# Reordered attention and delta-rule groups, and a last down panel in halves, in a two-layer decoder trunk

## The chip, the cores and the metric

The kernel runs on one core of one Trainium2 chip. The metric is the device time of one execution in microseconds, as the median of several. A profiled execution gives the trace: every instruction with its engine, start, duration, line and tiles, and what ended the idle time before it. The core has TensorE (matmuls, out of which results come in PSUM), VectorE, ScalarE, GpSimd (called POOL) and SyncE, which here issues the DMA transfers.

## What is computed

Two post-norm layers on 256 tokens of width 2048, in float32. Layer 0 mixes tokens by latent attention (12 heads, causal, low-rank queries and keys plus a rotary part), layer 1 by a chunked gated delta rule (12 heads, a short causal convolution on q, k, v). In both, 4 further heads attend to 256 memory tokens. One output projection takes all 16 heads, then come a norm, a squared-ReLU MLP of width 8192 and another norm.

```python
for i in range(2):
    mem_kv = mem @ mem_w_kv[i]
    h = x @ (mla_w_in if i == 0 else gdn_w_in)
    mix = mla_mixer(...) if i == 0 else gdn_mixer(...)      # 12 heads of 128
    mem_o = memory_attention(q_mem, mem_kv)                 # 4 heads of 128
    y = jnp.concatenate([mix, mem_o], -1) @ w_out[i]        # 2048 x 2048
    x = layer_norm(ALPHA * x + y, ln1_g[i], ln1_b[i])
    ff = jnp.square(jax.nn.relu(x @ mlp_w1[i])) @ mlp_w2[i] # 2048 x 8192 x 2048
    x = layer_norm(ALPHA * x + ff, ln2_g[i], ln2_b[i])

def gdn_mixer(...):
    qkv = silu(causal_depthwise_conv(h[..., :3 * MIX_WIDTH], conv_w))
    q, k = l2_normalize(q), l2_normalize(k)
    # per chunk of 64 tokens: u, w = solve(I + L, [v * beta, kb * exp(gc)])
    #   v_new = u - w @ state;  o = q_dec @ state + a_qk @ v_new
    #   state = state * g_last + k_dec^T @ v_new
    return rms_norm(o, o_norm) * silu(z)
```

## The kernel before

**Weights.** Every weight goes through the same ring. A chunk is 256 rows by 512 columns (two k-tiles of 128, 512 KB). SyncE loads it into one of four raw slots (`load`), ScalarE copies it to a reduced-precision high part `whi`, VectorE subtracts to get the low part `wlo` (both are called a split, `split` or `feed`), and TensorE multiplies high by high, high by low and low by high. Chunk c is split only when chunk c - 4 has been used (`chunk_used`), and loaded only when the split of chunk c - 4 is done (`lo_ready`). A panel is 512 output columns over all of k, mostly 8 chunks; panels alternate between two halves of PSUM, and `panel_free` says that one has been copied out. `panel_r` gives rows (tokens on partitions) with weights moving, 12 matmuls of 512 columns a chunk; `panel_t` gives columns, 24 matmuls of 256.

**Queues.** The five programs are written out by hand, one in-order queue for each engine, joined by counting semaphores. What stands behind a wait in a queue waits too.

**Layer 0's attention.** The panels qrope (2), qnope, knope, v (3 each, of two chunks) come from the normalised latents. POOL rotates the rotary queries. Then TensorE turns the rotated rows (L703), three times four transposes, each waiting for ScalarE's copy of the one before (`rot_out`), and starts `attention`: 16 heads in a pipeline of 19 steps. Step i has the scores of head i, one chunk of the first two out0 panels from step 5 on (`out0_chunk`), the transposes of head i-2's probabilities (`turn_probs`) and the values of head i-3 (`values`). ScalarE has `probs_out(i-2)`, `exps(i)`, `head_hi(i-3)` and a split; VectorE has `maxima(i)`, `divide(i-1)`, `head_lo(i-3)` and a split. Memory heads come last. out0's chunks take k-tiles in order, so each waits for the head just finished (`o_lo`).

**Layer 1's groups.** Four heads make a group, three groups. For each: panels q, k, v, with a convolution on each (`conv`: ScalarE scales a copy, VectorE adds three taps in 12 instructions of 253 to 255 columns, L1793, ScalarE takes tanh, VectorE multiplies, L1801, and TensorE turns the result back, `conv_turns`, L855); then `gdn(g)`: transposes of k, kb, q, a masked product, six levels of doubling that invert the triangular matrix, w and u, and four state steps (j loop), with the chunks of z and of the next q (or of qm1) put between (`beside`). At its end VectorE normalises the output rows `orow`, waits for POOL's rsqrt, scales them (`or_set`), and TensorE turns them (`turn`, L631). After the third group the memory heads of layer 1 run with six chunks of out1, once all turned rows are split.

**The end.** `mlp` has four groups of 4 up and 4 down panels. The last down panel ends token tile 0 and then tile 1 within each chunk; `last_rows` (VectorE) adds and takes sums, POOL computes the rsqrt of both tiles, VectorE the factors, ScalarE `norm_block` scales and shifts eight pieces of 512 columns, VectorE `finish` multiplies by the gain row and adds the shift row, and SyncE writes each piece out. The gain and shift rows `gb` are loaded last in SyncE's queue (`gain_rows`), after all weights:

```python
            mlp(1, "mlp1")
            sp.wait_ge(sem.z_ready, 3)
            gain_rows(ln2_g[1:2, :], ln2_b[1:2, :])
```

Of the kernel before, what the change touches and what calls it, by code (L numbers as in the profile page):

```python
# [52 lines left out]
PANEL = KT // CK  # L53
GROUPS = FF // D
# [41 lines left out]
def out_chunk(name, u, ci):  # L96


    if u < 2:
        return CHUNK_AT[name] + 2 * ci + u  # L100
    return CHUNK_AT[name] + u * PANEL + ci
# [11 lines left out]
def place(nc):  # L113
# [27 lines left out]
    b.stats, o = at("stats", [P, TT, 4, 6], F32, o)  # L141
# [87 lines left out]
    b.gb, o = at("gb", [P, 2, D], F32, o)  # L229
    b.low, o = at("low", [P, 2 * UP // 2, S], F32, o)  # L230
# [3 lines left out]
class Semaphores:  # L234


    def __init__(self, signal):
# [41 lines left out]
        self.fin = signal("fin")  # L279
        self.c_sum = signal("c_sum")  # L280
# [88 lines left out]
def build(nc, x, mem, positions_, mla_w_in, mla_q_norm, mla_w_uq, mla_kv_norm, mla_w_ukv, gdn_w_in, gdn_conv,  # L369
          gdn_a_log, gdn_dt_bias, gdn_o_norm, mem_w_kv, w_out, ln1_g, ln1_b, mlp_w1, mlp_w2, ln2_g, ln2_b, out):  # L370
    with ExitStack() as ctx:
# [6 lines left out]
        pt_ps, o_ps = quad_ps[1][:, 2, :], quad_ps[1][:, 3, :]  # L378
        block = ctx.enter_context(nc.Block())
# [13 lines left out]
        def _(sp):  # L393
# [48 lines left out]
            def mlp(l, name):  # L442
                c0 = CHUNK_AT[name]
                with sp.Fori(0, GROUPS) as g:
# [6 lines left out]
                    for u in range(UP):  # L451
                        for ci in range(PANEL):
                            load(c0 + (UP + u) * PANEL + ci,
                                 [(lambda slot: b.raw[:, slot],
                                   mlp_w2[l, bass.ds(g * D + ci * CK * P, CK * P), u * CN:(u + 1) * CN]
                                   .rearrange("(t p) n -> p t n", p=P))], g * GCH)

# [15 lines left out]
            for ci in range(PANEL):  # L473
                for u in range(2):
                    load(out_chunk("out0", u, ci), whole(w_out[0], ci * CK, slice(u * CN, (u + 1) * CN)))
# [27 lines left out]
            for j in range(4):  # L503
                for t in range(TT):
                    sp.wait_ge(sem.fin, 2 * j + t + 1)
# [6 lines left out]
        def _(pe):  # L512
# [111 lines left out]
            def turn(g, src, kts):  # L624

                if g >= 2:
                    pe.wait_ge(sem.turn_f, g - 1)
                for i in range(2):
                    for t in range(TT):
                        kt = kts + i  # L630
                        last = nc.tensor.transpose(turn_ps[g % 2][:, (i * TT + t) * P:(i * TT + t + 1) * P],  # L631
# [53 lines left out]
            for i in range(2):  # L685
                panel_r(PANEL_AT["qrope"] + i, CHUNK_AT["qrope"] + 2 * i, 2, b.ch, b.cl, after_turn("cq"), n=6 * ROPE)
            for i in range(3):
                panel_t(PANEL_AT["qnope"] + i, CHUNK_AT["qnope"] + 2 * i, 2, b.ch, b.cl, after_turn("cq"))
            for i in range(3):
                panel_t(PANEL_AT["knope"] + i, CHUNK_AT["knope"] + 2 * i, 2, b.ch[:, 4:8, :], b.cl[:, 4:8, :],  # L690
# [1454 lines left out]
```

## Time and profile before

| | |
|---|---|
| median of 3 runs | 2470.22 us (2469.14 to 2471.08) |
| profiled execution, its own time | 2471.89 us |
| its span, first to last instruction | 2470.1 us |
| TensorE busy | 2384.2 us (97%) |
| mean granted TensorE clock | 0.986 |
| first matmul of the last down panel's end, to the last instruction | 2452.3 to 2470.1 us |

The span is what the views of the trace cover; the execution's own time has 1.8 us around it. A row of a timeline is a start, a duration, the engine, the instruction and, in brackets, the idle time before it and what ended it. The ends of matmuls are modelled, so a stop of TensorE is a little longer from start to start than its row says. The granted clock is 1.0 at 2.4 GHz and 0.5 at 1.2 GHz.

### The profile page before, as it was taken

The numbers are of one execution on the slowest core, as the hardware profiler recorded it, in microseconds if no ns is written. First come the engines' busy times: TensorE is split into PE (matmuls) and PEld (weight loads), VectorE is DVE, ScalarE is ACT, GpSimd is POOL, SyncE is SP. The second block draws the span as 40 slices with busy tenths as digits, with TensorE's granted clock in tenths as the row PEclk, the third lists the DMA queues.
The fourth block names the chain that finished last, engine by engine and source line by source line (L and its number), as shares of the span: only waits on it lengthen the run. The fifth ranks groups of instructions, "written<-read, shape, count | busy, mean of one in ns | idle before, by whom it ended". The sixth has DMA issues, their size and how long they took to land.

```text
span 2470.1 us, 35483 instructions
## 1 busy us (share of the span) xinstructions
PE 2384.2 (97%) x13572; PEld 2078.7 (84%) x13577; DVE 1467.5 (59%) x1550; ACT 1071.8 (43%) x1340; POOL 247.9 (10%) x221
## 2 busy tenths in 40 slices
PE   8999989999999999999999999989899999999997
PEld 7897778888888888889899898978788888888885
DVE  6654567546555556577756757545865554555555
ACT  4455444434444444354535435333443443443443
POOL 0150001001000001000122320310010000000000
PEclk9999999999999999999999999999999999999999
DMA  6662456565566565655424324126455665656654
GB/s 233 188 187 94 137 172 200 199 193 188 192 185 196 192 191 182 200 190 162 137 69 139 108 79 154 60 90 226 140 188 195 184 196 196 187 190 195 188 191 158
DMA packets 234624, 417.10 MB, mean 169 GB/s; under 512 B 23761, under 2 KB 42474, under 8 KB 232938
## 3 DMA queue, kind: packets, MB, share of 16 engines
q1 hardware_dynamic: 233114, 410.73, 52.2%
q10 hardware_dynamic: 1360, 4.19, 0.4%
q8 instruction: 116, 1.90, 0.3%
q14 instruction: 34, 0.28, 0.0%
HBM read 412.77 MB, written 2.10 MB: 168 GB/s over the span
## 4 chain that ended last, share of the span: by engine, by line
PE 48%; issue 40%; DVE 5%; POOL 4%; ACT 2%; DMA 1%; SPq 0%; POOLq 0%; ACTq 0%; DVEq 0%
PE quad L563 10%; PE quad L592 6%; PE quad L590 6%; PE quad L591 6%; PE quad L566 5%; PE quad L534 3%; PE quad L536 3%; PE quad L538 3%; DVE cv L1793 2%; POOL hl L2070 1%; ACT whi L1036 1%; PE quad L947 1%; PE quad L934 1%; DVE wlo L1413 1%; PE quad L944 1%
## 5 line engine op out<-in xcount | busy, mean ns | idle before, releaser
L1413 DVE TENSOR_TENSOR wlo<-raw,whi 128x1024 fp32r<-128x1024 f32 x760 | 979.1, 1297 | 726.1 <-ACT whi L1036 724.0
L1036 ACT ACTIVATE whi<-raw 128x1024 fp32r<-128x1024 f32 x760 | 798.7, 1058 | 979.7 <-PE quad L592 525.8
L563 PE MATMUL quad<-xs,whi 128*128 128x512 f32 x2048 | 649.9, 397 | 7.4 <-DVE xs L1673 3.7
L590 PE MATMUL quad<-whi,hh 128*128 128x512 f32 x1344 | 528.9, 393 | 5.2 <-DVE hl L1548 3.7
L592 PE MATMUL quad<-whi,hl 128*128 128x512 f32 x1344 | 523.8, 390 | 0.0
L591 PE MATMUL quad<-wlo,hh 128*128 128x512 f32 x1344 | 523.5, 390 | 0.0
L566 PEld LDWEIGHTS quad<-xs,wlo 128*128 128x128 f32 x2048 | 386.7, 189 | 91.0
L566 PE MATMUL quad<-xs,wlo 128*128 128x256 f32 x2048 | 403.8, 279 | 0.0
L563 PEld LDWEIGHTS quad<-xs,whi 128*128 128x128 f32 x2048 | 314.6, 190 | 10.0 <-DVE wlo L1413 5.5
L590 PEld LDWEIGHTS quad<-whi,hh 128*128 128x128 f32 x1344 | 252.7, 188 | 60.0 <-issue 7.2
L592 PEld LDWEIGHTS quad<-whi,hl 128*128 128x128 f32 x1344 | 252.5, 188 | 53.1
L591 PEld LDWEIGHTS quad<-wlo,hh 128*128 128x128 f32 x1344 | 252.7, 188 | 51.8
L534 PE MATMUL quad<-xs,whi 128*128 128x256 f32 x704 | 203.5, 289 | 1.5 <-DVE wlo L1413 1.5
L2070 POOL TENSOR_TENSOR hl<-relu,hh 128x1024 fp32r<-128x1024 f32 x32 | 80.8, 2524 | 1193.2 <-ACT hh L1219 1193.2
L536 PE MATMUL quad<-xs,whi 128*128 128x256 f32 x704 | 200.0, 284 | 0.0
L538 PE MATMUL quad<-xs,wlo 128*128 128x256 f32 x704 | 199.9, 284 | 0.0
L534 PEld LDWEIGHTS quad<-xs,whi 128*128 128x128 f32 x704 | 135.8, 193 | 4.3 <-DVE wlo L1413 2.1
L536 PEld LDWEIGHTS quad<-xs,whi 128*128 128x128 f32 x704 | 135.9, 193 | 0.0
L538 PEld LDWEIGHTS quad<-xs,wlo 128*128 128x128 f32 x704 | 135.8, 193 | 0.0
L2102 POOL TENSOR_TENSOR qr<-nt,level 128x512 f32<-128x512 f32 x36 | 57.9, 1623 | 129.8 <-DVE nt L1850 78.0
L1702 DVE TENSOR_TENSOR relu<-quad,low 128x1024 f32<-128x1024 f32 x32 | 39.2, 1225 | 50.1 <-ACT low L1215 50.1
L590 PE MATMUL quad<-whi,xs 128*128 128x512 f32 x160 | 64.6, 404 | 0.0
(286 smaller groups left out, 2103.4 us busy)
## 6 DMA issues: line engine op xcount, KB each, us to landing
raw<-in_mlp_w SPq DMA_DIRECT2D x512, 512.0 KB
raw<-in_gdn_w_in SPq DMA_DIRECT2D x105, 512.0 KB
raw<-in_w_out SPq DMA_DIRECT2D x64, 512.0 KB
raw<-in_mem_w_kv SPq DMA_DIRECT2D x32, 512.0 KB
raw<-in_mla_w_in SPq DMA_DIRECT2D x25, 512.0 KB
raw<-in_mla_w_ukv SPq DMA_DIRECT2D x24, 256.0 KB
gb<-in_ln_g SPq DMA_DIRECT2D x4, 1024.0 KB, 6.5
gb<-in_ln_b SPq DMA_DIRECT2D x4, 1024.0 KB, 8.5
```

The lines of the kernel that those rows point to most:

```text
L534: nc.tensor.matmul(o, b.whi[:, slot, k, cols], ah[:, kt, :], start=start, stop=False, skip_group_check=True)
L536: nc.tensor.matmul(o, b.whi[:, slot, k, cols], al[:, kt, :], start=False, stop=False, skip_group_check=True)
L538: last = nc.tensor.matmul(o, b.wlo[:, slot, k, cols], ah[:, kt, :], start=False, stop=stop, skip_group_check=True)
L563: last = nc.tensor.matmul(both, b.whi[:, slot, k, cols], b.xs[:, :, kt, :], start=start, stop=stop, skip_group_check=True)
L566: last = nc.tensor.matmul(ps[:, j, S:2 * S], b.wlo[:, slot, k, cols], b.xh[:, kt, :], start=False, stop=False, skip_group_check=True)
L590: nc.tensor.matmul(ps[:, t, 0:n], ah[:, kt, toks], hi[:, k, 0:n], start=start, stop=False)
L591: nc.tensor.matmul(ps[:, t, 0:n], ah[:, kt, toks], lo[:, k, 0:n], start=False, stop=False)
L592: last = nc.tensor.matmul(ps[:, t, 0:n], al[:, kt, toks], hi[:, k, 0:n], start=False, stop=stop)
L1036: nc.scalar.activation(b.whi[:, c % NSPLIT], b.raw[:, slot], ACT.Copy).then_inc(sem.hi_ready, 1)
L1413: nc.vector.tensor_tensor(b.wlo[:, c % NSPLIT], b.raw[:, c % NRAW], b.whi[:, c % NSPLIT].bitcast(F32), ALU.subtract).then_inc(sem.lo_ready, 1)
L2070: nc.gpsimd.tensor_tensor(b.hl[:, 4 * u:4 * u + 4, :].rearrange("p k s -> p (k s)"), b.relu[:, u % 2, :], b.hh[:, 4 * u:4 * u + 4, :].rear ...
L2102: nc.gpsimd.tensor_tensor(b.bm[:, t], b.nt[:, t], b.level[:, l, :].unsqueeze(1).to_broadcast((P, GH, P)), ALU.mult).then_inc(sem.bm_set, 1)
```

## The change

- **Layer 0.** Memory heads come first (`head_tile` maps the pipeline's number to the tile of `hh`). The 11 latent panels no longer stand ahead of `attention`, but in its steps 0 to 6 (`LATENT_STEPS`); the rotated rows are turned in steps 2, 6 and 9, and the out0 chunks come from step 7 on, 12 beside the steps, in the order of k-tiles 12 to 15, then 0 to 11. Before `scores(0)` TensorE waits until VectorE has taken the ckv turns.
- **Groups.** `conv(g + 1, 0)` stands before the turned rows of group g on ScalarE and VectorE, with the scaling of `orow` inside it; TensorE has four k chunks instead of three before those turns; ScalarE copies kbt before the tanh of the v convolution; `conv(g, 1)` has a split between taps and tanh; the first chunk's `vn` is copied straight from PSUM, and TensorE waits for `uu` later.
- **Layer 1's attention.** The third group's rows are scaled and turned inside the pipeline (steps 0, 2, 3), into the bank of panel qm1; out1's chunks 0 to 3 need only the first two groups.
- **The end.** The last group is written out for SyncE and TensorE. Its last down panel is loaded and multiplied in halves of 256 columns: first half both token tiles, second half tile 0 over all four chunks, then tile 1. VectorE multiplies z by the gain ahead (`gained`, after each of the first three splits of that panel); per tile it takes sums, and the result is z times rs plus a shift. Tile 0's shift comes from VectorE, tile 1's from TensorE (`final_shift`: identity times the shift row plus a diagonal of the factors times the gain row). ScalarE's `norm_block(3, j)` and `finish` go. The output is written tile by tile.

```diff
+OUT0_ORDER = list(range(NH // CK, PANEL)) + list(range(NH // CK))
+def head_tile(n):
+    return NH + n if n < NM else n - NM
+LATENT_STEPS = {0: [("qrope", 0), ("qrope", 1)], 1: [("qnope", 0), ("qnope", 1)], 2: [("qnope", 2), ("knope", 0)],
+                3: [("knope", 1), ("knope", 2)], 4: [("v", 0)], 5: [("v", 1)], 6: [("v", 2)]}
+OUT0_STEP = len(LATENT_STEPS)
+OUT0_BESIDE = NH + NM + 3 - OUT0_STEP
+ROTATED_STEPS = [2, 6, 9]
...
# SyncE, last panel of the last group
+                            if final and u == UP - 1:
+                                n0 = u * CN + ci // HALF * S
+                                load(c0 + (UP + u) * PANEL + ci,
+                                     [(lambda slot: b.raw[:, slot].rearrange("p t (k n) -> p (t k) n", n=S),
+                                       mlp_w2[l, bass.ds(g * D + ci % HALF * 2 * CK * P, 2 * CK * P), n0:n0 + S]
+                                       .rearrange("(t p) n -> p t n", p=P))], g * GCH)
+                                continue
...
# TensorE, layer 0
-            pe.wait_ge(sem.rot_done, 3)
-            for g in range(3):
-                pe.wait_ge(sem.rot_out, g + 1)
...
+            pe.wait_ge(sem.turn_f, TURN_AT["ln1_0"])
...
+            def latent_step(i):
+                for name, k in LATENT_STEPS.get(i, []):
+                    latent_panel(name, k)
+                if i >= OUT0_STEP:
+                    out0_chunk(i - OUT0_STEP)
+                if i - 1 in ROTATED_STEPS:
+                    pe.wait_ge(sem.rot_out, ROTATED_STEPS.index(i - 1) + 2)
+            def rotated_step(i):
+                if i in ROTATED_STEPS:
+                    g = ROTATED_STEPS.index(i)
+                    pe.wait_ge(sem.pt_out, i - 1)
+                    turn_rotated(g)
...
# TensorE, last down panel
+            def final_panel(p, c0, poff, off):
+                ...
+                for ci in range(HALF):
+                    pe.wait_ge(sem.lo_ready, off + (c0 + ci + 1))
+                    for t in range(TT):
+                        last = part(ci, t)
+                    last.then_inc(sem.chunk_used, 1)
+                for ci in range(HALF, PANEL):
+                    pe.wait_ge(sem.lo_ready, off + (c0 + ci + 1))
+                    last = part(ci, 0)
+                last.then_inc(sem.half_rows, 1)
+                for ci in range(HALF, PANEL):
+                    part(ci, 1).then_inc(sem.chunk_used, 1)
+            def final_shift():
+                pe.wait_ge(sem.gb_in, 32 * 4)
+                for j in range(4):
+                    nc.tensor.matmul(shift_banks[j], b.ident[:, :], b.gb[:, 1, j * CN:(j + 1) * CN], start=True, stop=False)
+                pe.wait_ge(sem.diag_set, 1)
+                for j in range(4):
+                    nc.tensor.matmul(shift_banks[j], b.diag[:, :], b.gb[:, 0, j * CN:(j + 1) * CN], start=False,
+                                     stop=True).then_inc(sem.fin_a, 1)
...
# TensorE, groups
-                    pe.wait_ge(sem.d_u, n0 + t + 1)
...
+                    if j == 0:
+                        pe.wait_ge(sem.d_u, n0 + 1)
...
-                if g < HG - 1:
-                    turned_panel(f"k{g + 1}", 0, 3)
+                if g == HG - 1:
+                    return
+                turned_panel(f"k{g + 1}", 0, 4)
+                turn_rows(g, turn_ps)
...
# TensorE, layer 1's attention
+            def out1_step(i):
+                if i < NH // CK:
+                    out1_chunk(i)
+                if i == 1:
+                    pe.wait_ge(sem.a_o, HG * NC)
+                if i == 2:
+                    pe.wait_ge(sem.panel_free, PANEL_AT["qm1"] + 1)
+                    turn_rows(HG - 1, [panel_ps[PANEL_AT["qm1"] % 2][:, k, :] for k in range(2)])
...
# ScalarE
+                    for t in range(TT):
+                        act.wait_ge(sem.p_kbt, n0 + t + 1)
+                        bank_out(b.kbt, t, side_ps, sem.a_kbt)
                 conv(g, 2, keys_out)
-                for t in range(TT):
-                    act.wait_ge(sem.p_kbt, n0 + t + 1)
-                    bank_out(b.kbt, t, side_ps, sem.a_kbt)
...
+                conv(g + 1, 0, lambda: feed(1))
+                feed(1)
                 for k in range(2):
                     split_turn(TURN_AT[f"gdn{g}"] + k, b.hh, g * GH + 2 * k)
...
# VectorE, groups
+                dve.wait_ge(sem.p_u, n0 + 1)
+                nc.vector.tensor_copy(b.vn[0:CHUNK, 0].rearrange("p h c -> p (h c)"),
+                                      side_ps[0][0:CHUNK, :]).then_inc(sem.d_vn, 1)
...
+                conv(g + 1, 0, 1, scaled)
+                feed(1)
+                turned_out([turn_ps[(TURN_AT[f"gdn{g}"] + k) % 2] for k in range(2)])
...
# VectorE, last down panel
+                        if last_group and u == 2 * UP - 1 and j < UP - 1:
+                            dve.wait_ge(sem.gb_in, 32 * 4)
+                            dve.wait_ge(sem.lo_ready, off + (c0 + NSPLIT + u * PANEL + j + 1))
+                            for t in range(TT):
+                                gained(t, slice(j * CN, (j + 1) * CN))
...
+            def final_rows(name, u, halves, g):
+                ...
+                dve.wait_ge(sem.chunk_used, last_c - HALF)
+                for t in range(TT):
+                    link(rows(0, t))
+                    gained(t, cols[0])
+                dve.wait_ge(sem.half_rows, halves)
+                sums(0)
+                factor_of_mean(0)
+                for j in range(2):
+                    shift(j)
+                    scaled(0, j, b.shift[:, j % 2, 0:CN])
+                dve.wait_ge(sem.chunk_used, last_c)
+                sums(1)
+                for j in range(2, 4):
+                    shift(j)
+                    scaled(0, j, b.shift[:, j % 2, 0:CN])
+                factor_of_mean(1)
+                nc.vector.tensor_scalar(b.diag[:, :], b.ident[:, :], b.nmr[:, 1:2], None, ALU.mult).then_inc(sem.diag_set, 1)
+                for j in range(4):
+                    dve.wait_ge(sem.fin_a, j + 1)
+                    scaled(1, j, shift_banks[j])
```

## Rows read from the trace of the kernel before

**Rows 1.** The page: busy time of TensorE, and its granted clock in 40 slices, in tenths.

```profile
PE 2384.2 (97%) x13572; PEld 2078.7 (84%) x13577; DVE 1467.5 (59%) x1550; ACT 1071.8 (43%) x1340; POOL 247.9 (10%) x221
...
PEclk9999999999999999999999999999999999999999
```

**Rows 2.** What TensorE waited for: us in total, times, longest us.

```profile
PE quad L631 <- DVE z L1620: 11.6, 2, 5.8
...
PE quad L855 <- DVE cv L1801: 5.3, 2, 2.7
...
PE quad L590 <- DVE hl L1548: 3.7, 4, 1.0
...
PE quad L975 <- DVE qr L1890: 3.6, 3, 1.2
...
PE quad L902 <- ACT kbt L1321: 3.6, 3, 2.0
...
PE quad L934 <- DVE kt L1865: 1.7, 3, 0.6
...
PE quad L534 <- DVE wlo L1413: 1.5, 2, 1.1
...
PE quad L748 <- DVE hl L1548: 1.0, 1, 1.0
```

**Rows 3.** Busy time of each engine in five stretches, then granted clock and DMA.

```profile
195.00:297.00 102.00, 93.01 (x458) 76.05 (x461) 50.53 (x100) 49.22 (x122) 0.00 (x0) 0.97 0.28 93
1184.00:1619.00 435.00, 419.28 (x3170) 393.25 (x3170) 277.43 (x334) 182.56 (x316) 97.40 (x63) 0.98 0.34 105
1475.00:1500.00 25.00, 22.34 (x165) 22.13 (x164) 20.11 (x32) 12.97 (x33) 4.53 (x3) 0.86 0.48 148
1619.00:1665.00 46.00, 35.68 (x160) 29.27 (x159) 22.33 (x36) 17.93 (x36) 6.22 (x4) 0.89 0.27 92
2453.00:2470.10 17.10, 0.00 (x0) 0.00 (x0) 12.50 (x22) 5.75 (x8) 0.70 (x1) 0.65 0.32 123
```

**Rows 4.** Timeline 199 to 210: start, us, engine, what, [idle before and its end].

```profile
201.93 1.12 PE L703 MATMUL quad<-ident,qrrow 128*128 128x128 f32 x4 [2.23 <-ACT qrt L1147]
...
199.36 1.06 ACT L1036 ACTIVATE whi<-raw 128x1024 fp32r<-128x1024 f32 x1 [1.69 <-PE quad L592]
...
200.33 1.06 ACT L1143 ACTIVATE vrows<-quad 128x512 f32<-128x512 f32 x2
...
209.47 0.47 ACT L1155 ACTIVATE prob<-quad,mx 128x256 f32<-128x256 f32 x1 [2.69 <-DVE mx L1534]
```

**Rows 5.** Timeline 140 to 142, where the layer's latents are turned.

```profile
140.14 0.38 PE L682 MATMUL quad<-ident,krot 128*128 128x128 f32 x2
...
141.76 1.65 DVE L1435 TENSOR_SCALAR xf<-quad,vcol 128x256 f32<-128x256 f32 x4
```

**Rows 6.** Timeline of VectorE at the first border of two groups.

```profile
1307.63 1.23 DVE L1413 TENSOR_TENSOR wlo<-raw,whi 128x1024 fp32r<-128x1024 f32 x1
...
1322.01 5.00 DVE L1793 SCALAR_TENSOR_TENSOR cv<-quad,vcol,cv 128x253 f32<-128x253 f32 x12
```

**Rows 7.** Timeline of TensorE: two matmuls of 256 columns in a row.

```profile
1326.35 0.28 PE L536 MATMUL quad<-xs,whi 128*128 128x256 f32 x1
1326.47 0.28 PE L538 MATMUL quad<-xs,wlo 128*128 128x256 f32 x1
```

**Rows 8.** Timeline of VectorE in the last panel and after it.

```profile
2433.50 2.57 DVE L1413 TENSOR_TENSOR wlo<-raw,whi 128x1024 fp32r<-128x1024 f32 x2
...
2437.56 1.23 DVE L1413 TENSOR_TENSOR wlo<-raw,whi 128x1024 fp32r<-128x1024 f32 x1 [1.49 <-ACT whi L1036]
...
2457.69 0.69 DVE L1963 TENSOR_TENSOR z<-z,gb 128x512 f32<-128x512 f32 x1
```

**Rows 9.** The transfers of the last gain and shift rows, and their landing.

```profile
L440 SPq DMA_DIRECT2D gb<-in_ln_b x1: 424/424/424, 2435.9 to 2435.9; - x1
...
DMA to landing us min/median/max: 6.3/7.3/8.3
```

More of the change, by code:

```diff
@@ L229, in place @@
     b.gb, o = at("gb", [P, 2, D], F32, o)
+    b.shift = b.relu
+    b.diag, o = at("diag", [P, P], F32, o)
     b.low, o = at("low", [P, 2 * UP // 2, S], F32, o)
@@ L727, in key_blocks @@
             def key_blocks(n):
-                return [(kb, t) for kb in range(TT) for t in range(TT) if n >= NH or t >= kb]
+                return [(kb, t) for kb in range(TT) for t in range(TT) if not NM <= n < NM + NH or t >= kb]
             def turn_probs(n):
@@ L750, in values, with attention @@
                 last.then_inc(sem.o_done, 1)
-            def attention(n0, heads, between):
+            def attention(n0, heads, between, after=lambda i: None):
                 n = len(heads)
@@ L814, in mlp_group @@
+            def mlp_group(l, name, turned, g, done=0, after_chunk=None, final=False):
                 p0, c0 = PANEL_AT[name], CHUNK_AT[name]
@@ L1011, in _ @@
                     place = PANEL - 1 if i == 1 else PANEL // 2 + 1
-                    turned_panel(name, 3 if g and i == 1 else 0, place)
+                    turned_panel(name, 4 if g and i == 1 else 0, place)
                     conv_turns(g, i - 1)
@@ L1380, in _ @@
                 early = 3 if g else 0
-                feed(2 if g else 0)
-                conv(g, 0)
+                if g:
+                    feed(1)
+                else:
+                    conv(0, 0)
                 feed(PANEL - 1 - early)
@@ L1391, in _, with rows_hi @@
             take_t("qm1", 0, b.qm, 0, scale_mem)
-            attention(NH + NM, NM, 0, NH // CK)
+            def rows_hi(i):
+                if i == 3:
+                    for k in range(2):
+                        split_turn(TURN_AT[f"gdn{HG - 1}"] + k, b.hh, (HG - 1) * GH + 2 * k)
+            attention(NH + NM, NM, 0, NH // CK, rows_hi)
             feed(UP * PANEL - NH // CK)
@@ L1395, in _ @@
             mlp(1, "mlp1", True)
-            for j in range(4):
-                norm_block(3, j)
         @block.vector
@@ L1782, in _, with conv @@
                                   turn_ps[1][:, 0:NC * NH]).then_inc(sem.gcum_set, 1)
-            def conv(g, i, splits=0):
+            def conv(g, i, splits=0, between=lambda: None):
                 m = 3 * g + i
@@ L1798, in conv @@
                 last.then_inc(sem.conv1, 1)
+                between()
                 feed(splits)
@@ L1936, in _, with rows_step @@
                 conv(g, 2, 2)
-                gdn(g)
-            attention(NH + NM, NM, 0, NH // CK)
+                last_group = gdn(g)
+            def rows_step(i):
+                scaled, turned_out = last_group
+                if i == 0:
+                    scaled()
+                if i == 2:
+                    turned_out([panel_ps[PANEL_AT["qm1"] % 2][:, (TURN_AT[f"gdn{HG - 1}"] + k) % 2, :] for k in range(2)])
+            attention(NH + NM, NM, 0, NH // CK, rows_step)
             feed(PANEL - 1 - NH // CK)
```

288 lines of the change are left out of this document (186 added, 102 removed).

## The prediction

> **What bounds the kernel now.** I read the page first: TensorE is busy 97% of the span and its granted clock is almost always full [rows 1]. No other engine comes near, so the time is TensorE's work plus the places where it stands or runs at half clock, plus the tail. The change leaves TensorE's work almost as it is, so all it can win is such places. The list of TensorE's waits names them [rows 2], and windows price them [rows 3]. Four matter here:
> - layer 0's attention, 195 to 297: 9.0 us idle, and half clock for some 7 us (the mean clock of 0.97 over 102 us is 3.1 us short, twice that at half);
> - the delta-rule groups, 1184 to 1619: 15.7 us idle; the mean clock of 0.98 stands for some 17 us at half;
> - the group that ends layer 1's mixer and its attention, 1619 to 1665: 10.3 us idle, 10 us at half;
> - the end, 2453 to 2470: 17.1 us in which TensorE has nothing.
>
> The two norm waits (11.6 us, the first row of [rows 2]) stay. At half clock a busy microsecond gives half, so half-clock time costs half of its busy part.
>
> **Part 1, layer 0's attention in another order.** Removed: the three turns of rotated queries that wait for ScalarE's copies [rows 4], the chunks of out0 that wait for the head just finished (L1548, 3.7 us in rows, 5 or so with the steps that have no scores), and most of that half clock. Idle 9.0 plus half of about 5 busy us, 2.5, is 11.5. A stop also shows some 0.15 us short, because the row before it has a modelled end; with some 16 stops, 13.5 in all.
>
> Added, step by step, from how the same sequences run now. TensorE is through with the krot turns at 140.3, and `scores(0)` now needs turn_f of ckv, which VectorE finishes at 143.4 [rows 5]; before, only panels that don't need it stood there. That is 3.2 us. Step 2 turns the rotated queries behind `probs_out(0)`, which ScalarE reaches after a split and a panel's two copies. The same queue (split 1.06, copies 1.06, one more copy) now lets TensorE on at 201.93 after 2.23 us idle [rows 4], 2.4 between starts with the hidden part: 2.4. Step 6 is the same with 0.8 us of cover: 1.9. Step 4 needs the last knope panel copied: 2.2 after the panel's end, less 0.9 of turns and values, 1.4. Step 9 waits only for a copy of a head's probabilities, 0.4. Sum 9.3. Two of these stops are as long as ones that now end in half clock; I add 2 us for that. Part 1: -13.5 + 11.3, so **-2** (+2 if every stop brings half clock, -6 if none does and the ckv copy comes sooner).
>
> Nothing else should bind there: a latent step has 7 to 13 us of TensorE against 5 to 8 us of ScalarE (two to four splits of 1.06, copies of 1.06, two exps of 0.47 [rows 4]), and its splits are four chunks ahead. POOL's rotation of the queries, which was over before 199 while six more panels ran, gets two steps of two panels, some 25 us, to do the same.
>
> **Part 2, the delta-rule groups.** Three edits.
> - conv of the next q runs before the group's turned rows. Today the taps start at 1322.0, behind the turned rows and two splits, and TensorE waits for the result [rows 6]. Now they start behind the split that ends at 1308.9, take 5.0 as now, then `scaled` 1.2, a split 1.2 and the product: cv_set at about 1317.5, where TensorE needs it at 1326.6. The turns need or_set, 1315.2, at 1317.1: the fourth k chunk (2.9 us) is the cover, and without it they would wait 1 us. Queued behind the taps are the splits of k chunks 4, 5 and 6: done at 1316.4, 1318.7 and 1323.3, needed at 1317.9, 1320.8 and 1323.7. The last has 0.4 us to spare. Both stops go: 5.3 in rows, 5.7 with their hidden parts, and the half clock that follows the second (0.86 of 25 us, 3.5 [rows 3]). The split between taps and tanh removes the waits on L1413, 1.5.
> - The kbt copies stand before the tanh that waits for VectorE's taps: 3.6 us of L902's waits, 4.1 with their hidden parts, and 1.5 of clock. Next late is qd_set, within 0.5 us of when it is wanted: I keep 0.5.
> - The first chunk's vn straight from PSUM, before the uu copies: 3.6 in rows, and 1.36 each between starts, three times 4.1. Behind two of them stood 3.4 us of half clock, some 1.6 each; I count 2.5 of the 3.2.
>
> Sum 5.7 + 3.5 + 1.5 + 5.6 - 0.5 + 4.1 + 2.5 = 22.4, against 15.7 idle plus about 7 of clock in the window, of which only the 1.7 us on L1865 stay. **-22** (bounds -25, all gone, and -14, where the split with 0.4 us to spare is late and the clock still falls).
>
> **Part 3, layer 1's attention before the last rows' turns.** Before: 10.3 idle, and half of 6 busy us at half clock, 3: 13.4. Now TensorE waits only for the copy of qm1: a split and two copies, 2.4 (as in [rows 4]). The scaled rows come at 1625.8 but their turns only at 1633, behind three chunks. At step 4 the chunk wants POOL's low halves: ScalarE splits at step 3, 1636.9 to 1638.2, POOL needs 1.25 each, so 1640.2 where TensorE arrives at 1638.6: 1.6 idle. The end, with its wait of 1.0 at L748 [rows 2], stays. 5.3, and 1.1 for a clock drop as likely as not: **-7** (-9 to -4).
>
> **Part 4, the tail.** PE's last panel: a chunk now has 24 matmuls of 256 columns, 0.12 apart [rows 7], 2.88 us, in place of 2.72 (VectorE's splits follow each other at that pitch [rows 8]); all eight cost 1.3 more. Gained: when the first token tile is complete, 5.8 us of the second tile's matmuls cover its sums, factors and half its output; the variance and rsqrt chain of the second tile then overlaps outputs; VectorE's 16 passes of 0.69 over z [rows 8] become four adds of shift by TensorE and products made ahead. Alone this would end 5.3 us sooner: TensorE done at 2453.8, sums and factors 2458.8, first shift bank 2459.4, last product 2462.4, out 2.4 later.
>
> But `gained` waits for gb_in on VectorE, after the split of chunk 4, and the splits of chunks 5, 6 and 7 are queued behind it. SyncE issues ln_b at 2435.9, behind the last weights, and it lands 8.3 us later, at 2444.2 [rows 9]. Nothing in the change issues it earlier. The split of chunk 4 ends at 2436.2, so VectorE stands 8 us. Then each `gained` pair (1.25) and split (1.15) take turns: chunks 5, 6, 7 split at 2446.7, 2449.1, 2451.5. TensorE is at chunk 5 by 2443.7, waits 3.0, then about 1 at each of the next two. Tile 0 ends at 2453.1 and tile 1 at 2458.8, against 2452.5 for all of it now. From there VectorE: sums of tile 1 to 2460.5, two shift-and-product pairs to 2463.6, factors and diagonal to 2464.0, four TensorE products of one F32 row (0.5 to 1 us each, by clock), last output at 2467.5 to 2469; and 2.4 us to the end. Against 2470.1 that is 0 to +1.5; one more for half clock after the 3 us stop. Part 4: **+1.5** (-5.5 to +4).
>
> The stop on gb_in can be read with a page of the Trainium skill, which the sum doesn't need. "DMA: Bandwidth & Descriptors", section on the anatomy of one DMA, puts a transfer at about 2.0 us plus its bytes at 436 GB/s. By it, an estimate, the two rows of 1 MB would land 6.8 us after the first issue, at 2442.3, and the stop would be 1.1 us instead of 3.0. The trace's 8.3 decides; the weights of the last chunk are ahead of them in the same engines.
>
> At nothing: peeling the last group (its instructions are the same, and the loops show no wait), the order of out0's loads, the fifth stats slot, 1 KB rows in the last loads (each has 2.7 us, and chunks are loaded four ahead); if they were late, about 1 us a chunk.
>
> **Sum.** -2 - 22 - 7 + 1.5 = -29.5 of the profiled execution's 2471.9 (span 2470.1 and 1.8 around it), 2442.4. The median of the runs is 1.7 below that execution: **2440.7**, which I round to 2440.5.
>
> **Rivals.**
> - *The tail pays too.* If VectorE's wait for gb_in ends before chunk 5 is needed, part 4 is -5.3, not +1.5: 2434. For it: the landing is read from one execution. Against: it would have to come 5 us sooner, by 2439, when the split of chunk 5 could begin. 0.17.
> - *The group edits give half.* The taps ahead of the splits starve TensorE at k chunk 6 and v, or the clock falls elsewhere, since a stop of 2 us or less sometimes halves it and sometimes doesn't: part 2 is -11, 2451. For it: 0.4 us of slack. 0.15.
> - *Latent steps run in series (slower).* If each of the seven steps of part 1 waited for the whole ring (splits of both engines 2.3, copies 1.06, exps 0.9, and as much again for the probabilities' division and copy: some 5.7 us), part 1 would be +38 in place of -2: 2480. It decides from 4.5 us a step up. Against: a ring crosses two steps, and TensorE has 7 to 13 us in each. 0.02.
> - *No net change*: new stops of part 1 and 4 swell and the clock stays low, 2470. 0.03.
>
> Forecast as worked out: 0.63, itself 2434 to 2447.
>
> **How the numbers follow.** 2440.5 is the first case. The range 2428 to 2452 takes in the paid tail with parts 1 to 3 at their better bounds, and the half-paid groups. Measurements here tell 0.2%, 4.9 us, from no change: faster 0.94, same 0.03, slower 0.03.
>
> **What would show it.** TensorE stops at 140.3 (3.2), in steps 2, 4 and 6; no wait on L1801, L1890 or kbt, and no stop at the group borders; near 1619 a stop of 2.4 and one of 1.6; in the last panel one of 3 us ended by VectorE's split, with VectorE waiting for gb until some 8 us after its issue. I am wrong if the splits of the last panel aren't behind gb_in, if k chunk 6 waits for its split, or if stops of 2 to 3 us keep halving the clock.

## The result and the profile after

The changed kernel takes 2437.64 us (median of 4 runs, 2436.04 to 2440.71) against 2470.65 (4 runs, 2469.14 to 2472.87): ratio 0.9867, 95% interval 0.9850 to 0.9884. Forecast: 2440.5, range 2428 to 2452, faster. Run again later beside other kernels it took 2439.78 (2437.54 to 2443.65), ratio 0.9877 (0.9861 to 0.9894).

The profiled execution took 2436.78 us, its span is 35.0 us shorter. From its page: span, busy time of TensorE, and its granted clock in 40 slices.

```profile
span 2435.1 us, 35464 instructions
...
PE 2378.7 (98%) x13689; PEld 2078.4 (85%) x13689; DVE 1477.3 (61%) x1563; ACT 1065.9 (44%) x1332; POOL 247.1 (10%) x222
...
PEclk9999999999999999999999999999999999999999
```

TensorE is busy 98% of the span, 97% before [rows 1]. Its waits (us in total, times, longest):

```profile
PE quad L669 <- DVE z L1837: 11.6, 2, 5.8
...
PE quad L742 <- ACT probt L1304: 3.6, 2, 2.2
PE quad L913 <- DVE wlo L1573: 3.5, 3, 1.8
...
PE quad L758 <- DVE xf L1596: 3.0, 1, 3.0
...
PE quad L758 <- issue: 2.4, 1, 2.4
PE quad L937 <- DVE diag L1821: 1.8, 1, 1.8
PE quad L1065 <- DVE kt L2091: 1.7, 3, 0.6
...
PE quad L627 <- POOL hl L2225: 1.3, 1, 1.3
PE quad L787 <- DVE hl L1708: 1.0, 1, 1.0
...
PE quad L753 <- ACT kn L1205: 0.9, 1, 0.9
```

Against [rows 2]: the waits for the convolution (5.3), for the first chunk's rows (3.6) and for the kbt copies (3.6) are gone, and so are those for heads' hl in the chunks of out0. New are those that the prediction named, L758 twice (3.0 and 2.4), L742 (steps 2 and 6), L753 (step 4) and L627 <- POOL, one that it named with another size (L913, 3.5 where 3.0, 1 and 1 were forecast), and L937, the wait for the diagonal, which the forecast had inside the tail's chain. The norm (11.6) and L1065 (1.7) are as they were. Two more waits of the kernel before are gone, those of its last rows' turns and of the low halves behind them, which part 3 is about:

```profile
PE quad L631 <- DVE kb L1822: 6.0, 1, 6.0
...
PE quad L719 <- POOL hl L1995: 3.3, 1, 3.3
```

The stretches that answer to those of [rows 3], for TensorE alone: start and end, us, busy us, granted clock, DMA share, GB/s.

```profile
195.00:297.00 102.00, 98.81 (x500) 1.00 0.37 119
1067.00:1593.00 526.00, 520.25 (x3999) 1.00 0.40 121
1593.00:1640.00 47.00, 42.37 (x198) 1.00 0.40 136
```

The groups (second row) have a clock that rounds to full, 0.98 before. This row is longer than that of [rows 3]; between the same two landmarks (below), TensorE is idle 3.3 us of 523.3 here and was 17.4 us of 547.0 before. Of the 23.6 us that this stage is shorter, 14.0 are idle time, and 9.6 are busy time, most of it the 17.1 us at half clock that stood there before and that are gone.

**Where the time came from.** Starts of the same instruction in both traces cut the span into stages. This is how such a landmark looks, here the two that bound the groups (start, us, engine, line, and in brackets the idle time before it):

```profile
1069.63 0.55 PE L669 MATMUL quad<-ident,mrow 128*128 128x128 f32 x3 [2.38 <-DVE xf L1591]
...
1595.30 1.10 PE L758 MATMUL quad<-km,qm 128*128 128x256 f32 x4 [2.36 <-issue]
```

| stage, from and to | before | after | difference | predicted |
|---|---|---|---|---|
| start to the krot turn | 140.14 | 139.76 | -0.4 | 0 |
| to layer 0's first norm turn | 207.17 | 204.37 | -2.8 | -2 |
| layer 0's MLP, memory panels | 725.65 | 725.50 | -0.1 | 0 |
| groups, to where layer 1's attention would start | 546.95 | 523.31 | -23.6 | -22 |
| to layer 1's first norm turn | 116.51 | 108.02 | -8.5 | -7 |
| layer 1's MLP, to the last adds before the last panel | 694.55 | 694.49 | -0.1 | 0 |
| to the end | 39.13 | 39.65 | +0.5 | +1.5 |

The groups end, in both, where TensorE begins to wait: 1595.30 less 2.36 here, 1625.86 less 5.95 before.

**The tail.** VectorE from the last adds before the last panel, then what it does between the diagonal and the end:

```profile
2395.45 1.29 DVE L1729 TENSOR_TENSOR z<-quad,z 128x512 f32<-128x512 f32 x2 [0.34 <-PE quad L629]
...
2399.48 1.23 DVE L1573 TENSOR_TENSOR wlo<-raw,whi 128x1024 fp32r<-128x1024 f32 x1 [0.29 <-ACT whi L1177]
2407.71 1.29 DVE L1771 TENSOR_TENSOR z<-z,gb 128x512 f32<-128x512 f32 x2 [7.01 <-DMA gb<-in_ln_b]
2408.92 1.22 DVE L1573 TENSOR_TENSOR wlo<-raw,whi 128x1024 fp32r<-128x1024 f32 x1
2410.24 1.29 DVE L1771 TENSOR_TENSOR z<-z,gb 128x512 f32<-128x512 f32 x2
2411.45 1.22 DVE L1573 TENSOR_TENSOR wlo<-raw,whi 128x1024 fp32r<-128x1024 f32 x1
...
2427.63 0.29 DVE L1821 TENSOR_SCALAR diag<-ident,nmr 128x128 f32<-128x128 f32 x1
2429.13 3.32 DVE L1802 SCALAR_TENSOR_TENSOR z<-z,rs,quad 128x512 f32<-128x512 f32 x4 [1.22 <-PE quad L937]
```

VectorE stands 7.01 us for the gain rows (8 were forecast), and splits and products then take turns, as forecast. SyncE issued the rows here:

```profile
2399.65 0.48 SPq L462 DMA_DIRECT2D gb<-in_ln_g  x1
2400.17 0.43 SPq L463 DMA_DIRECT2D gb<-in_ln_b  x1
```

They are in 7.5 us behind the second issue, not 8.3 [rows 9], so TensorE stopped 2.0, 1.0 and 1.0 us from start to start instead of 3.0, 1 and 1. The estimate by the Trainium skill ("DMA: Bandwidth & Descriptors", anatomy of one DMA), 6.8 us from the first issue, was 1.3 short of the 8.1 measured. The page fits that line to single transfers issued by GpSimd; here SyncE issued two of them, behind loads in flight.

### The profile page after: what moved, and what is told of

Same layout as the page of the kernel before. It is cut to its first block, busy times and chain, and to the rows that moved or that the text cites. A ratio compares the mean times of both kernels' runs of the same rounds, so it can differ in the third digit from the quotient of the medians.

```text
span 2435.1 us, 35464 instructions
## 1 busy us (share of the span) xinstructions
PE 2378.7 (98%) x13689; PEld 2078.4 (85%) x13689; DVE 1477.3 (61%) x1563; ACT 1065.9 (44%) x1332; POOL 247.1 (10%) x222
## 4 chain that ended last, share of the span: by engine, by line
PE 83%; issue 11%; DVE 3%; POOL 2%; ACT 1%; DMA 1%; SPq 0%; ACTq 0%; DVEq 0%; POOLq 0%
PE quad L600 20%; PE quad L629 11%; PE quad L627 11%; PE quad L628 11%; PE quad L603 10%; PE quad L571 4%; PE quad L573 4%; PE quad L575 4%; PE quad L1078 1%; PE quad L1065 1%; PE quad L1075 1%; ACT whi L1177 1%; PE quad L669 1%; DMA raw<-in_mem_w_kv 1%; PE quad L1111 0%
## 5 line engine op out<-in xcount | busy, mean ns | idle before, releaser
L627 PE MATMUL quad<-whi,hh 128*128 128x512 f32 x1248 | 488.6, 392 | 2.2 <-POOL hl L2225 1.3
L629 PE MATMUL quad<-whi,hl 128*128 128x512 f32 x1248 | 485.8, 389 | 0.0
L628 PE MATMUL quad<-wlo,hh 128*128 128x512 f32 x1248 | 485.6, 389 | 0.0
L627 PEld LDWEIGHTS quad<-whi,hh 128*128 128x128 f32 x1248 | 234.3, 188 | 50.8 <-POOL hl L2225 1.7
L629 PEld LDWEIGHTS quad<-whi,hl 128*128 128x128 f32 x1248 | 234.2, 188 | 48.8
L628 PEld LDWEIGHTS quad<-wlo,hh 128*128 128x128 f32 x1248 | 234.3, 188 | 48.4
L627 PE MATMUL quad<-whi,xs 128*128 128x512 f32 x160 | 64.0, 400 | 0.0
```

Source lines behind the costliest of these rows:

```text
L627: nc.tensor.matmul(ps[:, t, 0:n], ah[:, kt, toks], hi[:, k, 0:n], start=start, stop=False)
L628: nc.tensor.matmul(ps[:, t, 0:n], ah[:, kt, toks], lo[:, k, 0:n], start=False, stop=False)
L629: last = nc.tensor.matmul(ps[:, t, 0:n], al[:, kt, toks], hi[:, k, 0:n], start=False, stop=stop)
```

## The experiments

All edits are made to the changed kernel. Ratios are to the kernel before, with 95% intervals; spans are of the profiled execution (after: 2435.1).

### Undoing the borders: the convolution behind the turned rows

```diff
-                conv(g + 1, 0, 1, scaled)
+                scaled()
                 feed(1)
                 turned_out([turn_ps[(TURN_AT[f"gdn{g}"] + k) % 2] for k in range(2)])
+                feed(2)
+                conv(g + 1, 0)
```

with ScalarE's queue to match, and three chunks of k ahead of the turns.

> The convolution of the next q stands behind the group's turned rows again, with three chunks of k ahead of the turns; the kbt copies and the first vn stay as changed. Theory: the two borders get their stops of 2.8 us back and the waits on the low halves of the weights, 5.7 and 1.5, and half clock after one of them, 3.5: 10.7 us, span 2445.8. Rival: the gain of the groups came from the kbt copies and the first vn, and the clock fell at the border only because those had stopped TensorE before: 5.7 or less, 2440.8 or less, and full clock behind the borders.

Measured: 2447.54 us, ratio 0.9904 (0.9887 to 0.9920), span 2445.1. TensorE at the first border:

```profile
1320.34 1.18 PE L986 MATMUL quad<-ident,cv 128*128 128x128 f32 x8 [2.67 <-DVE cv L2026]
```

Both stops are back as 2.67 us (2.83 from start to start), and behind the first TensorE ran 3.4 us at half clock (its clock is 0.87 from 1317 to 1330). The groups' stage grew by 7.6 us, 5.7 of stops and 1.7 of clock. The other 2.4 of the span lie in the last panel and belong to no border: VectorE stood 8.21 us for the gain rows instead of 7.01, and TensorE ran 6.8 us at half clock. The theory's place and stops were right, its clock share was too large: 7.6, not 10.7. The 1.5 for the low halves did not return (no wait for them in the groups); the split in k's convolution was not undone here (below).

### Undoing the kbt copies' place

```diff
-                    for t in range(TT):
-                        act.wait_ge(sem.p_kbt, n0 + t + 1)
-                        bank_out(b.kbt, t, side_ps, sem.a_kbt)
-
                 conv(g, 2, keys_out)
+                for t in range(TT):
+                    act.wait_ge(sem.p_kbt, n0 + t + 1)
+                    bank_out(b.kbt, t, side_ps, sem.a_kbt)
```

> ScalarE copies the turned scaled keys (kbt) behind the tanh of v's convolution again; all else stays as changed. Theory: TensorE waits for them in each of the three groups again, 1.36 us between starts, 4.1 in all, less what the now later qd_set takes, and the clock falls to half after some of the stops, up to 1.7 us each: span 2439.2 to 2440.9 against 2435.1. Rival: the group edits worked through the borders alone, and another order of ScalarE's copies is made good before TensorE asks: 2435 to 2436.

Measured: 2442.05 us, ratio 0.9882 (0.9867 to 0.9897), span 2441.3. The stop in the first group:

```profile
1212.04 1.10 PE L1033 MATMUL quad<-nt,ones 128*128 128x512 f32 x2 [0.71 <-ACT kbt L1471]
```

It is 0.71 us, not the 2.0 of [rows 2], and the groups' stage grew by 2.2 us only. The rest of the span's 6.2 is half clock in layer 0 (below) and in layer 1. The term was too large by more than half: the rest of the old wait needs another edit undone as well (all group edits together, below). No half clock came in the groups, where 1.5 us of it were forecast.

### Undoing the first vn

```diff
-                dve.wait_ge(sem.p_u, n0 + 1)
-                nc.vector.tensor_copy(b.vn[0:CHUNK, 0].rearrange("p h c -> p (h c)"),
-                                      side_ps[0][0:CHUNK, :]).then_inc(sem.d_vn, 1)
...
-                    if j:
+                    if j == 0:
+                        dve.wait_ge(sem.d_u, n0 + 1)
+                        nc.vector.tensor_copy(vn, uu).then_inc(sem.d_vn, 1)
+                    else:
```

and on TensorE the wait for both uu copies ahead of the chunk loop.

> The first chunk's vn is made from the uu copy again, and TensorE waits for both uu copies ahead of the chunk loop; all else stays as changed. Theory: three stops of 1.36 us come back, 4.1, and half clock behind two of them, 2.5 as predicted: 2441.7 against 2435.1. Rival: the half clock behind them in the kernel before belonged to a row of stops that now are gone, or is a matter of chance: 4.1 alone, 2439.2.

Measured: 2445.28 us, ratio 0.9899 (0.9882 to 0.9917), span 2441.0. The wait, and the clock behind the third stop:

```profile
PE quad L1108 <- DVE qr L2117: 3.6, 3, 1.2
```

```profile
1568.00:1580.00 12.00, 10.80 (x74) 0.86 0.12 41
```

Three stops of 1.36 us and 3.4 us at half clock behind one of them: the groups' stage grew by 5.6. Half clock can follow such a stop when the other stops around it are gone, but it followed one of three and not two, so the size lies between theory and rival. In two of the four executions the whole took some 5 us more (2447.88 and 2448.54 against 2442.68 and 2442.12); without a profile of them the place is open.

### Undoing the split in k's convolution

```diff
-                conv(g, 1, 1)
-                feed(4)
+                conv(g, 1)
+                feed(5)
```

and the like on ScalarE.

> Only the split between the taps and the tanh of k's convolution is undone (on ScalarE and on VectorE). Theory: TensorE waits for the low halves of one weight chunk of k or v in the second and third group again, 1.3 us at most each and 1.5 in all: span 2436.6. Rival: those waits belonged to the borders, which now leave the splits more room: 2435.1, no stop.

Measured: 2446.62 us (one run), span 2444.9; the groups' stage grew by 4.0, more than either theory gave. In the second group:

```profile
1339.33 0.39 PE L571 MATMUL quad<-xs,whi 128*128 128x256 f32 x1 [1.57 <-DVE wlo L1573]
```

TensorE waits for low halves three times (2.3 us in the list of waits) and once for qr (L1043, 0.7): what is queued behind the late split seems to be late too, more than the 1.5 of [rows 2]. That these stops come from this edit rests on one execution, but they stand in no profile that keeps the edit. The rest of the span's 9.8 lies elsewhere, 3 us of it half clock in layer 0.

### Undoing all group edits together

> All group edits undone together: the convolution of the next q behind the turned rows with three chunks of k ahead of them, the split between taps and tanh of k's convolution, the kbt copies and the first vn as before. Parts 1, 3 and 4 stay. Undone one by one, the borders gave back 7.6 us between the start of the groups and their end, the kbt copies 2.3 and the first vn 5.6, 15.5 in all, and the change gained 23.7 there. Theory: what is missing is half clock that comes back only where several stops stand together (17 us of it stood in the groups before, 7 in the three runs together): the stops alone give 12, the clock up to 8.5 and k's convolution 1.5: the stretch grows by 20 to 24, span 2455 to 2459. Rival: the edits are independent and the clock is a matter of chance with each stop: 15.5 and 1.5, span 2452.

Measured: 2461.87 us, ratio 0.9965 (0.9952 to 0.9977), span 2458.4. Its two landmarks and its waits:

```profile
1072.25 0.66 PE L669 MATMUL quad<-ident,mrow 128*128 128x128 f32 x4 [2.39 <-DVE xf L1591]
...
1616.73 2.05 PE L758 MATMUL quad<-km,qm 128*128 128x256 f32 x4 [2.36 <-issue]
```

```profile
PE quad L986 <- DVE cv L2027: 5.3, 2, 2.7
...
PE quad L1108 <- DVE qr L2116: 3.6, 3, 1.2
...
PE quad L1033 <- ACT kbt L1472: 3.1, 3, 1.8
```

The groups' stage is 18.8 us longer than after. One by one the four edits gave 7.6, 2.2, 5.6 and 4.0, 19.4. So they are nearly independent in sum, but not each by itself: with all undone the kbt wait of the first group is 1.8, near the 2.0 of [rows 2], where its own edit gave 0.7, and the waits for low halves are 0.3, where the k edit alone gave 2.3. Which other edit makes the kbt wait long is not shown; the k edit is the likely one. By medians all of this is 22 to 24 us, of the 31 to 33 of the whole change. Against the kernel before 4.8 us are missing. 3.4 of them are clock: before, TensorE ran 17.1 us at half in this stage, here 10.2. The last 1.4 have a place in the lists of waits: the one for a low half behind the first border (1.1 of the 1.5 of [rows 2]) did not come back, and the kbt waits are 3.1 against 3.6. Why is open.

### Without the fourth k chunk as cover

```diff
-                turned_panel(f"k{g + 1}", 0, 4)
+                turned_panel(f"k{g + 1}", 0, 3)
```

> Three chunks of the next k stand ahead of the turned rows, and one behind them, in place of four ahead. Theory: the fourth chunk is the cover for the factor of the rows, without it the turns wait about 1 us at each of the two borders: two stops, span 2437.1 against 2435.1. Rival: the rows are ready by then, no stop, 2435.1.

Measured: 2442.85 us (one run), span 2441.1; the groups' stage is 1.8 us longer, from two stops like this one:

```profile
1308.67 1.09 PE L669 MATMUL quad<-ident,kb 128*128 128x128 f32 x8 [0.72 <-DVE kb L2048]
```

0.72 us where 1 was worked out (0.89 from start to start). The cover is real, in this one execution. Most of the rest of the span is half clock elsewhere, in layer 0 and layer 1's attention.

### The qrope panels ahead of the first scores

```diff
+            for k in range(2):
+                latent_panel("qrope", k)
             pe.wait_ge(sem.const_set, 2)
             pe.wait_ge(sem.turn_f, TURN_AT["ln1_0"])
```

> The two panels of rotated query parts stand ahead of the first head's scores again (on all three engines), the other latent panels stay in steps 1 to 6. Theory: they cover VectorE's copy of the turned latent rows; the stop of 3.15 us at 139.9 goes and with it the half clock from 143.0 to 146.4 (1.7 us): span 2430.2 against 2435.1. Rival A: the half clock comes with the first heads' small matmuls, whatever stood before: only 3.15, 2432. Rival B: the stop moves, since the rotated turns of step 2 now have one step less before them: 2435.

Measured: 2434.95 us, ratio 0.9857 (0.9840 to 0.9873), span 2432.3. The stop is gone, L758 <- DVE xf stands in no wait, the clock from 139 to 152 is full, and the stage from the krot turn to the first norm turn is 199.6 us against 204.4: -4.8, as the theory had it. No stop moved: L742's 3.6 are unchanged. The other half-clock rival, that it comes with the small matmuls whatever stood before, did not hold here; but full clock behind this place also came in two of ten profiles with the stop in (below), so of the 4.8 only the 3.15 are sure. 1.5 us were lost again in the last panel, where VectorE stood 8.55 us for the gain rows instead of 7.01.

### The gain rows early

```diff
+                                if ci == 0:
+                                    sp.wait_ge(sem.z_ready, 3)
+                                    gain_rows(ln2_g[1:2, :], ln2_b[1:2, :])
```

ahead of the last panel's loads, and removed behind them.

> The two gain rows of the last norm (2 MB into SBUF) are requested ahead of the weights of the last down panel instead of behind them; nothing else differs from the changed kernel. Theory: VectorE's 7.0 us wait for them, with the splits of chunks 5 to 7 queued behind it, is all that stops TensorE in the last panel (2.0, 1.0 and 1.0 us between starts). All three stops go: span 2431.1 against 2435.1. Rival A: the 2 MB take the engines from the weights, which are read four chunks, some 11 us, ahead: one stop of up to 7 us moves into the panel before, and the span is 2435 to 2439. Rival B: the stops come from VectorE's two added products between two splits (1.4 us in 2.9): the last two stops stay and the span is 2433.

Measured: 2434.66 us, ratio 0.9848 (0.9832 to 0.9865), span 2435.4. SyncE's issues, and VectorE in the last panel:

```profile
2382.60 0.45 SPq L462 DMA_DIRECT2D gb<-in_ln_g  x1
2383.09 0.43 SPq L463 DMA_DIRECT2D gb<-in_ln_b  x1
```

```profile
2404.19 1.23 DVE L1573 TENSOR_TENSOR wlo<-raw,whi 128x1024 fp32r<-128x1024 f32 x1 [0.29 <-ACT whi L1177]
2405.52 1.29 DVE L1771 TENSOR_TENSOR z<-z,gb 128x512 f32<-128x512 f32 x2
```

VectorE does not wait for the rows, TensorE has no wait at L913, and from the last adds to the end it takes 35.2 us against 39.65: -4.4. The added products alone stop nobody, so rival B falls. Of rival A a part came: a weight load was late, and ScalarE's split waited for it,

```profile
2393.77 1.06 ACT L1177 ACTIVATE whi<-raw 128x1024 fp32r<-128x1024 f32 x1 [3.37 <-DMA raw<-in_mlp_w]
```

and VectorE's split behind it 3.20 us, where the changed kernel has no such wait. It reached no matmul: TensorE is busy without a break from 2376 to 2420, as the splits were chunks ahead. The span hides the gain, since this execution had 4.7 us more ahead of the last panel, most of it half clock again; the stage and the ratio (0.9848 against 0.9867 and 0.9877) show it.

### The tail as before

Here the last panel, the last norm and the stores are those of before.

> The changed kernel with the last panel, the last norm and the order of the stores as before; parts 1 to 3 stay. Theory: part 4 cost 0.5 us (the tails measured 39.35 and 39.87 us), so the span is 2434.6, the same within 1 us. Rival: the tail before gained or lost with the state that parts 1 to 3 leave (the clock in the last panel): 2432 or 2438.

Measured: 2437.59 us, ratio 0.9869 (0.9851 to 0.9887), span 2433.3. From the last adds to the end 39.35 us against 39.65 after and 39.13 before. (The expectation counts both tails from 0.22 us earlier; its 39.35 is the kernel before.) Part 4 cost 0.3 to 0.5 us in this execution, and 1.8 to 2.0 in another of the same kernel, whose tail took 41.1 (below); with the gain rows early it is worth 4.

### The changed kernel once more

> The changed kernel once more, unaltered, to see which of its half-clock stretches come again. Theory: the stops repeat to 0.1 us, and the half clock behind the stop of 3.15 us at 139.9 comes in some executions only: it stood in five of the six profiles with that stop, as 3.4 us in three and as 6.8 in two. Then the span is 2433.4 to 2437 with all else the same. Rival: the execution is the same in all, 2435.1.

(The expectation miscounts: it was five of seven.) Measured: 2439.78 us, as told above, span 2438.2. The groups' stage repeats to 0.1 us. What differs is the clock, and the wait for the gain rows, 8.52 us instead of 7.01:

```profile
2410.83 1.29 DVE L1771 TENSOR_TENSOR z<-z,gb 128x512 f32<-128x512 f32 x2 [8.52 <-DMA gb<-in_ln_b]
```

The tail is 41.1 us instead of 39.65, 1.5 more, and the wait is 1.5 longer. This holds from one profile to the next. In nine profiles with this tail and the rows asked for last, the rows came 7.5 to 9.1 us behind the second issue, VectorE waited 6.99 to 8.55, and in eight of them the tail was 32.6 us more than the wait, within 0.05. So the 3.4 us of half clock in the last panel here cost nothing of their own. The ninth is the one with the old convolution: 6.8 us of half clock, and 1.2 more than its wait explains.

The clock behind the stops of 3.15 and 2.39 us in layer 0's attention (granted clock 139 to 152 and 179 to 192, fifth number of a row), in four kernels that are alike up to there. After:

```profile
139.00:152.00 13.00, 10.01 (x52) 0.87 0.32 87
179.00:192.00 13.00, 10.77 (x87) 1.00 0.43 123
```

The same kernel again:

```profile
139.00:152.00 13.00, 10.01 (x52) 0.87 0.33 91
179.00:192.00 13.00, 10.77 (x75) 0.87 0.33 96
```

With the kbt copies as before, and with the old tail:

```profile
139.00:152.00 13.00, 10.01 (x46) 0.74 0.31 87
179.00:192.00 13.00, 10.77 (x75) 0.87 0.41 118
```

```profile
139.00:152.00 13.00, 10.01 (x61) 1.00 0.47 124
179.00:192.00 13.00, 12.11 (x98) 1.00 0.44 129
```

0.87 of 13 us is 3.4 us at half clock, 0.74 is 6.8. In ten profiles with the stop at 139.9 the clock behind it was 0.87 in five, 0.74 in three and full in two; behind the one at 181, 0.87 in six and full in four.

### All together

The changed kernel with the two edits that paid, and five more: rotated queries turned one step later and ahead of that step's panels (`ROTATED_STEPS = [3, 7, 10]`), head 4 waiting for its own k panel only (`ready=PANEL_AT["knope"] + h // 4 + 1`), `out1_chunk(0)` ahead of layer 1's first scores, the last rows turned in step 1 instead of 2, and the diagonal ahead of the last shift.

> The changed kernel with the gain rows early, the qrope panels first, and more: the rotated queries are turned one step later, ahead of that step's panels or chunk (2.4 and 1.6 us), head 4 waits for its own k panel only (1.1), the first chunk of layer 1's out1 stands ahead of its first scores (2.5), the last rows are turned a step sooner (1.6), and the diagonal of the last norm is made before the last shift (1.4). Theory: the stops are independent and each goes: 4.0 + 4.9 + 2.4 + 1.6 + 1.1 + 2.5 + 1.6 + 1.4 = 19.5, span 2416 against 2435.1. Rival: some stops only hide the next one, ScalarE's ring of copies above all, and half comes: 2425.

Measured: 2421.19 us (5 runs, 2419.33 to 2423.95), ratio 0.9799 (0.9785 to 0.9812), span 2419.5. It beats both kernels. L758, L753, L627 <- POOL and L913 are gone from TensorE's waits. Left, beside the norm's 11.6, are among others:

```profile
PE quad L669 <- DVE xf L1590: 3.5, 2, 2.4
...
PE quad L742 <- ACT probt L1303: 1.4, 1, 1.4
...
PE quad L935 <- DVE diag L1819: 0.2, 1, 0.2
```

Layer 0's attention takes 196.0 us (204.4), the tail 33.9 (39.65), and from the groups to layer 1's norm 628.9 (631.3), the last although 3.4 us at half clock stood at their start:

```profile
1060.00:1073.00 13.00, 10.62 (x77) 0.87 0.32 101
```

15.6 of the 19.5 us came in this execution, nearer to the theory than to the rival's half. The missing 3.9 are accounted for, with 0.6 won elsewhere: a stop of 1.4 that is left at L742 in step 3, 1.4 in layer 0's MLP and memory panels, where a second stop on the turned memory rows (1.15 us, at 1050) is new, and 1.7 for that half clock. The edits were made together, so their shares are read from the stages.

## Why the prediction was right

- **Part 1, -2: -2.8.** The stops came where they were named: 3.15 for 3.2, 2.39 for 2.4, 1.63 for 1.9, and in step 4 1.1 for 1.4. Step 9's didn't show. The 2 us for half clock were 1.7. That the first stop goes with the qrope panels is shown (-4.8 for it and its half clock). The rest of part 1 was not undone. A slip: 11.5 and 16 times 0.15 are 13.9, not 13.5, which would have made it -2.6.
- **Part 2, -22: -23.6.** The total is shown by undoing it (18.8, and 4.8 that no edit brought back, 3.4 of it clock). Within it three terms were mis-sized, with signs that cancel: the borders 7.6 instead of 9.2, since 3.4 us at half clock came back, which cost 1.7, and not 3.5; the kbt copies 2.2 instead of 5.1; the split in k's convolution 4.0 instead of 1.5. So that the total of part 2 is this near is in part luck. The step that failed in the last two is reading each row of the list of waits as the price of the edit that names its tile: a wait can also grow with whatever made the queue ahead of it late. The first group's wait for kbt is 0.7 us with only its own edit undone and 1.8 with all four. The first vn was 5.6 for 6.6.
- **Part 3, -7: -8.5.** Stops of 2.5, 1.6 and 1.3 us as forecast (2.4, 1.6, 1.0), and the 1.1 for a clock drop did not come, in this execution; in others of the same stage it did, 3.4 us at half for 1.7. No run undid this part: it rests on the stage's length and on the waits of 6.0 and 3.3 us that are gone.
- **Part 4, +1.5: +0.5.** The place and the queue behind the wait were right. The terms that were off are the landing of the rows, 7.5 us in place of 8.3, and the extra microsecond for half clock. The first is chance: the same rows took 9.1 in the second execution, whose tail was 41.1 us. The second is at nothing: half clock stood there in that execution, and the tail grew by the wait alone. (By the forecast's own times the end was to come at -0.2 to +1.3, not 0 to +1.5.) Without the wait the tail is 3.9 us shorter than before (35.2 against 39.1), where the forecast had 5.3. The missing 1.4 is the diagonal at the end of VectorE's queue, which TensorE's products and then VectorE itself wait for: with it one shift earlier the tail is 33.9, 5.3 shorter, in the kernel with all edits.
- The rivals: the tail paid only when the rows were issued earlier; the group edits did not give half; the latent steps did not run in series, since layer 0's stage is 2.8 us shorter and not 38 longer.

Sum: -29.5 forecast, -35.0 in spans and -33.0 and -30.7 in the medians of two sets. Of the 5.5 us between the first two, 2.1 are clock drops that were counted in parts 3 and 4 and did not come in this execution; the rest are the sizes above.

## What to carry to other kernels

When a change rests on an operand that arrives by DMA, find the issue in its queue: here the whole value of a rebuilt tail hung on two requests that stood behind the last weights, and moving them by eight loads gave 4.4 us. Price a stop from the stage it stands in, and undo edits alone and together: the wait list names the tile that was late, not what made it late. Where spans differ by 2 to 5 us, compare landmarks, not ends: of the 3.1 us between two executions of one kernel here, 1.6 were half clock in layer 0 and 1.5 the landing of the gain rows.

## What the runs showed of the hardware

- The same stop, in programs alike up to it, was followed by full clock, 3.4 or 6.8 us of half clock (the counts above). Of the three stops of 1.4 us at the first vn, two were followed by it in the kernel before and one in each of the two runs that brought them back; stops of 2.5 us at layer 1's first scores were in four of eleven profiles. In the attention and group stages it cost 1.5 to 1.7 us for each 3.4; in the last panel, hidden behind VectorE's wait, 3.4 us of it cost nothing.
- Two broadcasts of 1 MB were there 7.5 us behind the second issue in one execution and 9.1 in another, the same kernel, with the same loads ahead of them. Issued ahead of eight loads of 512 KB they were there after 8.7, and one of the loads came late enough to hold ScalarE 3.4 us; TensorE did not stop, with the splits chunks ahead.
